# Joints around seven-product pairs in a fused three-block kernel: side loads, held banks, residual steps and final tiles in another order

## What is computed

```python
def swiglu(h, w1, w2):
    g, u = jnp.split(h @ w1, 2, axis=-1)
    return (jax.nn.silu(g) * u) @ w2
# second block, per layer
x = x + FFN_RES_WEIGHT * _swiglu(_rmsnorm(x, ffn1_norm[layer]), ffn1_w_gate_up[layer], ffn1_w_down[layer])
x = x + _hybrid_mixer(...)
x = x + FFN_RES_WEIGHT * _swiglu(_rmsnorm(x, ffn2_norm[layer]), ffn2_w_gate_up[layer], ffn2_w_down[layer])
```

## Time and profile before

| | us |
|---|---|
| median of the three runs | 3530.12 |
| the profiled execution, its own time | 3532.91 |
| its span, first to last instruction | 3531.1 |
| PE busy | 3348.2 (95%) |
| DVE, POOL, ACT busy | 1901.6, 1630.4, 1470.9 |

### The profile page before, as it was taken

How to read it: one execution, slowest core, us unless ns; L and a number is a source line. 1 busy time by engine, 2 the same in 40 slices (tenths; PEclk the granted TensorE clock), 3 DMA queues, 4 the chain that set the end, 5 groups by cost and what they waited for, 6 DMA issues and landing times.

```text
span 3531.1 us, 47177 instructions
## 1 busy us (share of the span) xinstructions
PE 3348.2 (95%) x18766; PEld 2828.2 (80%) x18766; DVE 1901.6 (54%) x3348; ACT 1470.9 (42%) x2582; POOL 1630.4 (46%) x952
## 2 busy tenths in 40 slices
PE   8999999999999889999998999899999988999998
PEld 5767788877778779797776989799887768989776
DVE  3266766622331468173565836674553767636655
ACT  4533324523222355154455524453343655424543
POOL 3313455563344347464524645455445335645332
PEclk9999999999999989999999999999999999999999
DMA  7212233432343323233312232223233112323221
GB/s 272 68 48 66 97 99 127 160 122 85 135 136 116 128 76 105 87 108 107 90 33 73 99 107 94 80 100 106 88 111 106 44 57 91 110 87 107 73 66 54
DMA packets 102217, 345.95 MB, mean 98 GB/s; under 512 B 12173, under 2 KB 12557, under 8 KB 101838
## 3 DMA queue, kind: packets, MB, share of 16 engines
q1 hardware_dynamic: 101200, 341.10, 30.1%
q10 hardware_dynamic: 798, 1.85, 0.1%
HBM read 336.08 MB, written 2.10 MB: 96 GB/s over the span
## 4 chain that ended last, share of the span: by engine, by line
PE 80%; DVE 9%; ACT 5%; DMA 3%; POOL 2%; issue 1%; SPq 0%; DVEq 0%; ACTq 0%
PE ps L1398 14%; PE ps L1399 13%; PE ps L1400 13%; PE ps L1433 8%; PE ps L1435 8%; PE ps L1434 8%; PE ps L1458 2%; PE ps L1459 2%; PE ps L1460 2%; PE ps L1730 2%; DVE t L2451 1%; DMA t<-in_w_ffi 1%; PE ps L1757 1%; POOL t L3079 1%; DMA t<-in_w_ada 1%
## 5 line engine op out<-in xcount | busy, mean ns | idle before, releaser
L3079 POOL TENSOR_TENSOR t<-t,t 128x1024 fp32r<-128x1024 f32 (+2 forms) x408 | 921.7, 2265 | 1336.0 <-ACT t L1817 1323.5
L1398 PE MATMUL ps<-t,t 128*128 128x512 f32 x2608 | 1052.9, 404 | 71.6 <-POOL t L3079 61.1
L1399 PE MATMUL ps<-t,t 128*128 128x512 f32 x2608 | 1028.1, 394 | 0.0
L1400 PE MATMUL ps<-t,t 128*128 128x512 f32 x2608 | 1026.1, 393 | 0.0
L3089 POOL TENSOR_TENSOR t<-t,t 128x512 fp32r<-128x512 f32 x440 | 569.7, 1321 | 430.7 <-ACT t L1832 430.3
L1433 PE MATMUL ps<-t,t 128*128 128x256 f32 x2464 | 707.7, 287 | 47.7 <-DVE t L2327 15.3
L1434 PE MATMUL ps<-t,t 128*128 128x256 f32 x2464 | 702.4, 285 | 0.0
L1435 PE MATMUL ps<-t,t 128*128 128x256 f32 x2464 | 701.9, 285 | 0.0
L1398 PEld LDWEIGHTS ps<-t,t 128*128 128x128 f32 x2608 | 495.9, 190 | 208.2 <-issue 50.3
L1817 ACT CAST t<-t 128x1024 fp32r<-128x1024 f32 (+2 forms) x412 | 400.7, 975 | 541.8 <-PE ps L1400 304.0
L1400 PEld LDWEIGHTS ps<-t,t 128*128 128x128 f32 x2608 | 495.2, 190 | 110.1
(11 more groups left out here) (331 smaller groups left out, 3750.4 us busy)
## 6 DMA issues: line engine op xcount, KB each, us to landing
t<-in_w_f1i SPq DMA_DIRECT2D x88, 512.0 KB, 3.8
t<-in_w_f2i SPq DMA_DIRECT2D x88, 512.0 KB, 3.7
t<-in_w_ada SPq DMA_DIRECT2D x72, 512.0 KB, 3.7
t<-in_w_ffi SPq DMA_DIRECT2D x44, 512.0 KB, 5.4
t<-in_w_f1o SPq DMA_DIRECT2D x32, 512.0 KB, 4.0
t<-in_w_f2o SPq DMA_DIRECT2D x32, 512.0 KB, 4.1
t<-in_w_gate SPq DMA_DIRECT2D x24, 512.0 KB, 4.1
t<-in_w_out SPq DMA_DIRECT2D x48, 256.0 KB, 2.6
```

Of the source, the lines that this page charges most:

```text
L1398: e.matmul(out, wh[:, at], X.hi[c][:, 0:N], start=c == first, stop=False)
L1399: e.matmul(out, wh[:, at], X.lo[c][:, 0:N], start=False, stop=False)
L1400: m = e.matmul(out, wl[:, at], X.hi[c][:, 0:N], start=False, stop=c == final)
L3079: e.tensor_tensor(k.WL[k.slot[n]][:, 0:w], k.raw[:, j % NRAW, 0:w], f(k.WH[k.slot[n]][:, 0:w]), ALU.subtract).then_inc(*k.rest.inc(('rest' ...
```

## The change

- Side loads: `plain` takes one step per middle tile instead of two; the down-projection loop of part 0 takes two per tile and that of part 1 one for each of its first four tiles.
- Down-projection loop: `T(n)` now comes before `begin_pair` of the same n.
- Residual in split steps (`renew`): the scaling of x, sum_parts, squares, sum_highs and sum_lows are separate steps; the lows of tile n - 1 stand after residual(n), S1 is prepared at n = 5, S2 and S3 at n = 6.
- Banks: G, G, H and Q are held (`pass_on` hands a held bank to the next key without a wait), and of pair 0 both A and C.
- First pair (`first_products`): p6 and p7 run for inputs 0 to 2, then for 3; `roots` follows p4, `row` follows p3, all of pair 1's weights are prepared inside pair 0, and `pair_gate(0)` moves ahead of `first_copy(1)`.
- The first block's final tiles (`final_tile`, 8 DVE instructions) move from pairs 4 to 11 into the loop of part 0.
- The squares' ring has three buffers (`short`); the fourth is that of `first_copy`, which now waits for the last x tile and not for the last square.

```diff
@@ -114,6 +114,11 @@
         self.at[key], self.prior[key] = (i, before)
         return before
 
+    def pass_on(self, before, key):
+        i = self.at[before]
+        self.key[i] = key
+        self.at[key], self.prior[key] = (i, before)
+
     def let(self, key):
         i = self.at[key]
...
@@ -613,7 +623,7 @@
     m = Norm(res.sum, k.X, lambda j: ('x', 'out1', j), A, lambda j: k.sm[:, j:j + 1], lambda j: k.ada[:, 24 + j:25 + j], [('filled', ('out1', 7)), ('gain2',)], keep=True, bank=True)
     for j in range(11):
         norm(on, m, j)
-    twin = banked(Sum('f1_0', k.R[0], S, ('normed', 'n2', 7), range(8), 0, [('lo', ('mid', 'ff1'), FF - 1)]))
+    twin = short(banked(Sum('f1_0', k.R[0], S, ('normed', 'n2', 7), range(8), 0, [('lo', ('mid', 'ff1'), FF - 1)])))
...
@@ -670,18 +680,24 @@
         (plain if m.scale is None else fours)(on, m, first, count)
         after = (m.next, 0) if part else (None if m.scale is None else m, first + count)
         for n in range(KT):
-            if after[0] is not None:
+            on.T(('ed'[part], m.tag, n), m.wo, n, m.mid, kt=count, first=first)
+            for _ in range(n < 4 if part else 2):
+                next(m.side, None)
+            key = ('ed'[part], m.tag, n)
+            if part == 0:
+                if m.whole is not None:
+                    on.final_tile(m.whole, n, 'final_g')
                 begin_pair(on, *after, n)
-            on.T(('ed'[part], m.tag, n), m.wo, n, m.mid, kt=count, first=first)
-            if part:
-                on.residual(m.res, n, ('d', m.tag, n), ('filled', ('u', m.tag, FF - 1)))
+                on.partial(m.res, n, key)
+            elif m.res.four:
+                renew(on, m.res, n, key, ('filled', ('u', m.tag, FF - 1)), *after)
             else:
-                on.partial(m.res, n, ('e', m.tag, n))
+                on.residual(m.res, n, key, ('filled', ('u', m.tag, FF - 1)))
 
...
 def begin_pair(on, m, i, n):
 
-    if n == KT - 2:
+    if m is not None and n == KT - 2:
         on.sums(m, i, 'S1')
         on.round(m, i, 'A11')
...
@@ -689,11 +705,43 @@
         on.minus(m, i, 'S1')
...
+    if m is not None and n == KT - 1:
         on.sums(m, i, 'S3')
         on.minus(m, i, 'S2')
         on.round(m, i, 'S3')
         on.minus(m, i, 'S3')
+
+
+def renew(on, res, n, key, since, m, i):
+
+    on.residual(res, n, key, since)
+    if 0 < n < 7:
+        on.sum_lows(res, n - 1)
+    on.sum_parts(res, n)
+    if n < 6:
+        on.squares(res, n)
+        on.add_squares(res, n)
+    on.sum_highs(res, n)
+    if n == 5:
+        on.sums(m, i, 'S1')
+        on.round(m, i, 'A11')
+        on.round(m, i, 'S1')
+        on.minus(m, i, 'A11')
+        on.minus(m, i, 'S1')
+    if n == 6:
+        on.sums(m, i, 'S2')
+        on.sum_lows(res, n)
+        on.round(m, i, 'S2')
+        on.minus(m, i, 'S2')
+        on.sums(m, i, 'S3')
+        on.round(m, i, 'S3')
+        on.minus(m, i, 'S3')
+        on.squares(res, n)
+    if n == 7:
+        on.sum_lows(res, n)
+        on.add_squares(res, 6)
+        on.squares(res, n)
+        on.add_squares(res, n)
 
...
+def first_products(on, m):
+
+    for j in m.before.later:
+        on.last_lows(m.before, j)
+    for js in ((0, 1, 2), (3,)):
+        on.product(m, 0, 'p6', js)
+        on.product(m, 0, 'p7', js)
+    on.second_sum(m, 0)
+    on.third_sum(m, 0)
+    on.minus(m, 1, 'S1')
+    on.product(m, 0, 'p4')
+    on.up_sum(m, 0)
+    on.sums(m, 1, 'S2')
+    on.round(m, 1, 'S2')
+    on.roots(m.scale, 4 if m.whole else 2)
+    on.product(m, 0, 'p2')
+    on.sums(m, 1, 'S3')
+    on.round(m, 1, 'S3')
+    on.round(m, 1, 'A22')
+    on.minus(m, 1, 'S2')
+    on.minus(m, 1, 'S3')
+    on.minus(m, 1, 'A22')
+    on.round(m, 1, 'A12')
+    on.minus(m, 1, 'A12')
+    on.product(m, 0, 'p3')
+    on.row(m.scale)
+    on.sums(m, 1, 'S4')
+    on.round(m, 1, 'S4')
+    on.minus(m, 1, 'S4')
 
...
 def fours(on, m, first, count):
@@ -719,8 +798,7 @@
         on.product(m, i, 'p1')
         if not begin:
             on.last_sum(m, i - 1)
-            if i > 1:
-                on.pair_gate(m, i - 1)
+            on.pair_gate(m, i - 1)
         on.first_copy(m, i)
         if begin:
             on.round(m, i, 'A22')
@@ -734,31 +812,23 @@
             on.round(m, i + 1, 'A11')
             on.minus(m, i + 1, 'A11')
         on.product(m, i, 'p5')
-        if i == 1:
-            on.row(m.scale)
-            on.pair_gate(m, 0)
         if more:
             on.sums(m, i + 1, 'S1')
             on.round(m, i + 1, 'S1')
+        if i == 0:
+            first_products(on, m)
+            continue
         if not begin:
             on.pair_up(m, i - 1)
         if more:
             on.minus(m, i + 1, 'S1')
             on.sums(m, i + 1, 'S2')
             on.round(m, i + 1, 'S2')
-        if i == 0:
-            for j in m.before.later:
-                on.last_lows(m.before, j)
...
@@ -786,8 +854,6 @@
             on.roots(m.whole.sum, 1)
         if m.whole is not None and i == 3:
             on.row(m.whole.sum)
-        if m.whole is not None and 4 <= i < 12:
-            on.final_tile(m.whole, i - 4, 'final_g')
     on.last_sum(m, final)
...
     res.later = (0, 1, 2, 3)
     for n in range(KT):
-        begin_pair(on, m, 0, n)
         on.T(('out2_' + L, n), 'out' + L, n, at.OA, kt=4)
-        on.residual(res, n, ('out2_' + L, n), ('filled', ('fqk', L, 7)))
+        renew(on, res, n, ('out2_' + L, n), ('filled', ('fqk', L, 7)), m, 0)
     scale = res.sum
-    nxt = banked(Sum('fin2' if layer else 'f1_1', k.R[1 - layer], S, ('fox', L, 7), range(8) if layer else (), 2, [('lo', ('mid', 'f2_' + L), FF - 1)]))
+    nxt = banked(Sum('fin2' if layer else 'f1_1', k.R[1 - layer], S, ('fox', L, 7), range(8) if layer else (), 2 if layer else 0, [('lo', ('mid', 'f2_' + L), FF - 1)]))
+    if not layer:
...
-        out = (self.take(k.banks, *key, hold=i == 0 and bank == 'A') if opens and js[0] == 0 else self.bank(*key))[:, col:col + 256]
+        out = (self.take(k.banks, *key, hold=i == 0 and bank in 'AC') if opens and js[0] == 0 else self.bank(*key))[:, col:col + 256]
         if i == 1 and p == 'p6':
             k.banks.let(('A', m.tag, 0))
+            k.banks.let(('C', m.tag, 0))
         self.wait_ge('rest', m.tag, i, piece)
...
 
         if piece == 'S1':
-            self.k.banks.take(('Q', m.tag, i))
+            self.k.banks.take(('Q', m.tag, i), True)
+        if piece == 'S4':
+            self.k.banks.let(('Q', m.tag, i))
 
...
 
     def residual(self, res, n, key, since=None):
-        if res.four:
-            self.k.banks.take(('GH'[n % 2], res.A.tag, n // 2))
+        if not res.four:
+            self.add_squares(res, n)
+
+    def sum_parts(self, res, n):
+
+        banks, tag, j = (self.k.banks, res.A.tag, n // 2)
+        if n in (0, 1, 2):
+            banks.take(('GH'[n % 2], tag, j), True)
+        else:
+            banks.pass_on(('H', tag, j - 1) if n % 2 else ('G', tag, j - 2), ('GH'[n % 2], tag, j))
+
...
@@ -1837,7 +1922,7 @@
         if i:
             self.wait_ge('last sum', m.tag, i - 1)
         else:
-            self.wait_ge('ssq', m.scale.tag, 7)
+            self.wait_ge('x', m.before.tag, 7)
         e.copy(k.tmp[3][:, 0:256], self.bank('A', m.tag, i)[:, 0:256]).then_inc(*k.act.inc(('first copy', m.tag, i)))
```

89 lines of the change are left out of this document (52 added, 37 removed).

## The result

The changed kernel takes 3423.01 us (median of four runs, 3418.28 to 3425.88) against 3529.22 us before: a ratio of 0.9693, 95% interval 0.9675 to 0.9711, that is 106 us less. The forecast was 3424.5 us. The profiled executions' own times are 3532.91 and 3425.88 us, 107.0 apart, so the traces can be compared term by term.

The account below looks back on a forecast made before the run. PE, busy 95% of the span, was taken as the bound, with only its idle time and slow starts winnable. Terms 29 + 22 + 16.4 + 12.2 + 26 = 105.6 us gave 3427.3, less 2.8 for the median: 3424.5 us, range 3397 to 3466.

Parts of the forecast that it names:

- Side loads: In ff1, spreading them ends all but one of PE's waits for POOL's low weight parts and restores the clock: 29 us.
- rival (b): Side loads only change place: SP's queue stands in the down-projections instead, they win nothing, 3453 us; chance 0.10.
- The cover of 3 us: In ff1, the chain to the next gate weights takes 12.8 us, needed after 16.2 us, so 3 us remain.
- Passages: Part 0 to part 1, four times: rounding T(7)'s weights first removes PE's wait of 4.14 us each; 22 us, ends 16 and 24.
- the clock: At the passage into part 1, clock 0.77 over a 15 us stretch: about 2 us of work lost.
- Joints out of ff1 and f2_0: From T(6)'s end to p7 of pair 1, bank waits go, some DVE lateness stays: 16.4 and 12.2 us.
- Out of out2: Two joints: p3 starts at 15 instead of 9.5 us; 12.7 each plus 0.3 each in the eight tiles, 26 us.
- rival (a): In the joints, DVE's chain takes the place of the banks as what delays PE; joints at 27, 3452 us; chance 0.24.
- the full (c): More than forecast: all of 31.6, 24.4 and 77.5 us won, 3397 us; 3405 if nine tenths; chance 0.08.
- (d): Slower: held banks leave one for a joint's T, each waiting for the lows before; 22 us slower, 3552; chance 0.05.
- (e): `first_products` still waits for `row` on DVE, so only ff1 and the passages are won, 3478 us; chance 0.03.
- The wait for `up_sum` of 2 to 6 us: Expected sign in the changed kernel's profile: PE waits this long for `up_sum` in each of four joints.

Follow-up runs that it names:

- side_only: The kernel before with only the side loads spread as in the change; 3499.4 us, ratio 0.9896 to the kernel before.
- side_pairs: The changed kernel with two side loads in a row at every odd middle tile of ff1, none at even ones; 3426.3 us, ratio 0.9710 to the kernel before.

## Why the prediction was right

**Total.** 3424.5 us forecast, 3423.0 measured, and each term is within 4 us. That the total came within 1.5 us is partly luck: the named places gave 112.3 us, 6.7 more than the 105.6 of the sum, and the rest of the program, for which the forecast had nothing, took 4.2 back.

**Side loads** (29 forecast, 31.7 measured). The total and the place were right, and rival (b) is excluded by side_only. The step behind it, a gate load that waits for the second side unit of the tile before, is what the trace of before shows (898.22 and 898.24 us above), and by the same count side_pairs should hardly wait. What failed was my expectation of side_pairs, 12 to 18 us for any two side loads in a row, for which I had not counted the ring again. The cover of 3 us that the prediction worked out was not measured by itself.

**Passages** (22 and at most 24 forecast; 26.0 measured). The mechanism was right, and the trace of before has a wait of 4.1 us in each of the four. The mis-sized term is the clock: I took 2 us of lost work for it from one stretch at 0.77, and 2.4 us off the sum without a reason. 4 x 4.14 = 16.6 us were waiting, and 9.4 us faster matmuls, 2.4 each on average (2.6, 3.2, 1.8 and 1.8: the same wait does not cost the same).

**Joints out of ff1 and f2_0** (16.4 and 12.2; 17.2 and 14.0). From the end of T(7) at 1219.29 to the end of `up_sum` at 1230.41 + 0.69 = 1231.10 are 11.8 us, what the prediction summed from single instructions. PE had meanwhile lost 1.05 us to the low part of the last tile and 0.62 to POOL, so that `up_sum` itself cost it 0.35 and not 2.3. A later wait for `up_sum`, that of pair 1, cost 1.35, and `row` waited 1.33 for the root. The waits are more and smaller than forecast. The clock stayed at 1.00; I had set 2.2 us aside for it and a later wait together.

**Out of out2** (26; 23.4). Here the split was wrong. Of out2_0's 11.9 us only 35.2 - 27.1 = 8.1 lie in the joint, where I had 12.7, and some 4 in the eight tiles, where I had 0.3. The rows of the changed kernel's timeline that tell it (POOL's squares and low parts, last_lows on DVE, p4, p3):

```profile
1845.13 2.75 POOL L3203 TENSOR_TENSOR t<-t,t 128x512 f32<-128x512 f32 x2
...
1847.83 6.77 POOL L3189 TENSOR_TENSOR t<-t,t 128x512 fp32r<-128x512 f32 x4
1848.35 6.80 DVE L2875 SCALAR_TENSOR_TENSOR t<-t,t,t 128x512 fp32r<-128x512 f32 x4
...
1849.60 0.57 PE L1501 MATMUL ps<-t,t 128*128 128x256 f32 x1 [2.16 <-POOL t L3189]
...
1857.29 0.36 PE L1501 MATMUL ps<-t,t 128*128 128x256 f32 x1 [1.47 <-DVE ps L2475]
```

p3 starts 1857.29 - 1838.41 = 18.9 us after T(7), not 15. The four last_lows take 6.8 us, 1.70 each; at the shortest of the earlier trace rows, 0.74, they would be 3.0, at its median 3.8. The 15 us had no term for them that can be read off, and left the longer ones to rival (a). And p4 waits 2.16 us (3.5 in out2_1) for POOL's low part of A22, which stands behind two squares: a queue that I had not followed past the joint's DVE chain.

**The rivals and the signs.** (a) did not occur by its own sign: PE's largest wait in a joint is for `up_sum` out of ff1 and f2_0 (1.4 and 1.5 us) and for POOL's low part out of out2 (2.2 and 3.5). What it said of `last_lows` came true out of out2. (b) is answered above. Of the full (c) the side loads and the passages reached their parts, the joints not: 54.6 us of 77.5, to 0.1 us what was forecast for them together, with the two kinds of joint off in opposite directions. (Nine tenths of (c) would be 3410, not 3405.) (d) and (e) did not occur. No T in a joint waits for a bank. The wait for `up_sum` of 2 to 6 us in each joint did not come: two waits, 1.7 to 2.9 us together, in three joints, one of 0.5 in the last. The clock came to 1.00 in two of the joints and to 0.94 out of out2_0, as forecast, but stayed at 0.81 out of out2_1, behind a wait of 3.49 us for POOL; there the forecast of above 0.9 failed. The waits on POOL's 1024-wide parts fell to 11.3 us, where about 20 were forecast.

## What to carry to other kernels

Where several engines run fixed orders, a wait is often not set by speed but by what stands in front: a bank handed out in turn to the wrong product (19 us for one hold), a rounding ahead of the weights of the product before (26 us at four places for one line moved). Sum the chain of the engine that is late next, instruction by instruction, and every queue that feeds the same products, not the busiest one only. And when loads of two kinds share a ring, count for each load which unit it waits for, and count again for every new order: two side loads in a row cost 31.7 us at every tile and 2.7 at every second one.
